# A dense expert stage on one Trainium2 core: VectorE takes every third weight tile's low part instead of every second

## The chip, the cores and the metric

The kernel runs on one NeuronCore of a Trainium2 chip. The metric is the device time of one execution in microseconds (us), median over runs. The profile is of one execution, with times from the start of its span.

Engines: TensorE (PE) multiplies, VectorE (DVE), ScalarE (ACT) and GpSimd (POOL) do elementwise work, SyncE (SP) issues most DMAs. GpSimd also issues the indirect DMAs, which gather rows.

## The reference

Two layers in fp32 on 512 tokens (528 with 16 meta tokens) of width 1024. The first is latent attention beside a convolution, then a feed-forward layer with 16,384 experts; the second mixes sparse latent attention with a recurrent branch. The time around the change goes into the experts:

```
q = (xb @ wq).reshape(C, 8, 2, 64)
s = einsum('chpd,hpnd->chpn', q, keys)          # 8 heads, two halves, 128 keys each
sv, si = top_k(s, 16)                           # then the best 16 of the 16 x 16 sums
g = softmax(top_s)                              # 16 gates for each head
act = gelu(einsum('chkd,cd->chk', u_tab[eidx], xb))
out = einsum('chk,chkd->cd', g * act, v_tab[eidx])
```

Each token uses 128 of the 16,384 rows of u_tab and v_tab.

## The kernel before

**Two ways for the experts.** For the first 128 tokens (and partly for 16 more) the kernel gathers the chosen rows: GpSimd issues an indirect DMA of 128 rows of 1024 numbers (line 2838) into one of six buffers `fetched`, and VectorE multiplies and adds it up. One such row step is a "pick". For the other 368 tokens it computes all experts densely: U products (activations of 128 experts), a gelu on ScalarE, a gating on VectorE (line 2426, times the scattered gates `gr`), and V products. A group is 1024 experts: 8 U tiles and 8 V tiles. There are 16 groups. The U products of nine of them were made earlier and their activations spilled to HBM; SyncE loads these back. In the dense stage the U and V products of group n+1 and n alternate where group n+1 is not spilled (here called a UV stretch, 16 products), and V products stand alone where it is (a V stretch, 8 or 16 products). The stage has 184 products, tiles 100 to 283 of one stream of weight tiles.

**Three-pass products.** A weight tile has 128 x 1024 numbers. SyncE loads it to one of four buffers `wraw`. ScalarE casts it to the high part `wh` (fp32r, line 1330), and another engine makes the low part `wl` = `wraw` - `wh` (one of three buffers each). TensorE then does, for each of eight slices, high x high, high x low and low x high (lines 515 to 517): 24 matmuls. The moving operand of a V product is the gated activations, split in the same way: ScalarE casts WTH (line 1652), VectorE subtracts to get WTL (line 1917, the same helper as for `wl`).

**Who makes the low part.** `on_vector(n)` says whether tile n is VectorE's. `low_of(n)` gives the semaphore that TensorE and SyncE wait on, `w_lo_dve` or `w_lo`. VectorE's `split_lo` (line 1919) and GpSimd's (line 2714) both run through the tiles and each skips the other's.

**What orders the work.** Each engine goes through the same list of steps (`EXPERTS`), in order, waiting on semaphores:

- ScalarE: the high part of tile n waits for the load and for the end of product n-3, whose buffers it takes. It stands in order behind WTH casts and gelus.
- GpSimd: at product p the low part of tile p+2, if it is its own (waits for the high part), and then the gathers of that step, asked for four picks ahead (`LEAD`), each after the pick that last used the buffer.
- VectorE: at product p the low part of tile p+2, if its own; at a V product it then waits for the product's end, adds it to `h`, makes one or two WTL of the next group, and does the picks (`PICKS_AT`: about 1.7 for a product in UV stretches, 1.2 in V stretches). At a U step it does the gating.
- SyncE: the load of tile n waits for the low part of tile n-4.
- TensorE: product n waits for high and low part of tile n; the first V product of a group also for WTH and WTL.

Of the kernel before, what the change touches and what calls it, by code (L numbers as in the profile page):

```python
# [58 lines left out]
W_IN, W_OUT, W_Q, W_SPILL, W_EXP = 0, 12, 20, 28, 28 + 8 * SPILLED  # L59
W_IDX = W_EXP + 8 * (N_GROUPS - SPILLED) + 8 * N_GROUPS  # L60
# [82 lines left out]
def build_program(nc, hT, wstream, gains, consts, trig, w_uq, w_ukv, keys, w_uk, w_uv, w_rg, u_rows, v_rows, out):  # L143
# [319 lines left out]

    def on_vector(n):

        return n < 3 or W_EXP + 10 <= n < W_IDX and n % 2 == 1

    def low_of(n):
        return (w_lo_dve if on_vector(n) else w_lo).at(n)
# [1415 lines left out]
    def vector(dve):  # L1885
# [33 lines left out]
        def split_lo(n):  # L1919
            if on_vector(n):  # L1920
                dve.wait_ge(*w_hi.at(n))
                minus_high(wl[n % NSPLIT][:, :], wraw[n % NRAW][:, :], wh[n % NSPLIT][:, :]).then_inc(*w_lo_dve.tell(n))
# [785 lines left out]
    def gpsimd(pool):  # L2708
# [5 lines left out]
        def split_lo(n):  # L2714
            if n >= N_TILES:
                return
            s, r = n % NSPLIT, n % NRAW
            if on_vector(n):
                return
            pool.wait_ge(*w_hi.at(n))  # L2720
            minus_high(wl[s][:, :], wraw[r][:, :], wh[s][:, :]).then_inc(*w_lo.tell(n))
# [422 lines left out]
```

## Time and profile before

| | |
|---|---|
| median of 3 runs | 2054.63 us (2053.85 to 2056.38) |
| the profiled execution | 2055.25 us, span 2053.3 us |
| TensorE busy | 2016.6 us (98%) |
| VectorE busy | 1508.6 us (73%) |
| ScalarE busy | 994.3 us (48%) |
| GpSimd busy | 1049.1 us (51%) |

Engine busy times are sums of the spans of their instructions. Matmuls overlap, so a busy TensorE may still lose a little; its stalls are seen in its timeline as the idle time in brackets. An instruction that is held up by another engine on a shared resource is shown as busy and long, not as waiting.

### The profile page before, as it was taken

How to read it: one execution, taken by the hardware profiler on the slowest of the kernel's cores; microseconds unless marked ns; L12 is line 12 of the kernel's file. 1: busy time of each engine (PE TensorE's matmuls, PEld its weight loads, DVE VectorE, ACT ScalarE, POOL GpSimd, SP SyncE). 2: the span in 40 equal slices, each digit the busy share in tenths (PEclk: the TensorE clock that was granted, in tenths of full speed). 3: DMA queues.
4: the chain of work that ended last, by engine and by line, in shares of the span. 5: the costliest groups of instructions: out<-in, count | busy, mean ns of one | idle time of the engine just before them, and what ended most of it. 6: DMA issues, size and time to landing. Idle time of an engine off the chain costs nothing.

```text
span 2053.3 us, 31764 instructions
## 1 busy us (share of the span) xinstructions
PE 2016.6 (98%) x11815; PEld 1804.4 (88%) x11815; DVE 1508.6 (73%) x2840; ACT 994.3 (48%) x1825; POOL 1049.1 (51%) x615
## 2 busy tenths in 40 slices
PE   9999999999999999999999999999999999999998
PEld 8746789999999999999999999999867787877777
DVE  6237548979898479999989999997687645067863
ACT  4337433367789743333333343334556642255643
POOL 3213456764445567776767676673334444411242
PEclk9999999999999999999999999999999999999999
DMA  5330225776678899999999999996312222210021
GB/s 205 81 101 11 76 90 160 252 248 226 216 261 287 312 360 372 378 386 374 355 366 366 380 379 391 354 397 209 123 62 93 88 87 103 95 40 31 21 83 62
DMA packets 152855, 435.31 MB, mean 212 GB/s; under 512 B 14464, under 2 KB 62720, under 8 KB 150528
## 3 DMA queue, kind: packets, MB, share of 16 engines
q1 hardware_dynamic: 111232, 282.29, 38.9%
q0 software_dynamic: 41472, 151.01, 19.6%
q8 instruction: 95, 1.56, 0.3%
q14 instruction: 56, 0.46, 0.1%
HBM read 391.28 MB, written 41.97 MB: 211 GB/s over the span
## 4 chain that ended last, share of the span: by engine, by line
PE 83%; DVE 9%; issue 3%; DMA 2%; ACT 2%; POOL 1%; SPq 0%; DVEq 0%; ACTq 0%
PE bank L515 17%; PE bank L516 16%; PE bank L517 16%; PE bank L921 4%; PE bank L922 4%; PE bank L923 4%; PE bank L902 3%; PE bank L1142 2%; DVE wide L2390 2%; PE bank L690 1%; DMA fetched<-in_v_rows,diag 1%; DVE fetched L2370 1%; PE wide L1165 1%; PE wide L1153 1%; PE bank L1165 1%
## 5 line engine op out<-in xcount | busy, mean ns | idle before, releaser
L2712 POOL TENSOR_TENSOR wl<-wraw,wh 128x1024 fp32r<-128x1024 f32 x272 | 673.7, 2481 | 714.0 <-ACT wh L1330 712.4
L1330 ACT CAST wh<-wraw 128x1024 fp32r<-128x1024 f32 x360 | 375.2, 1045 | 167.2 <-PE bank L517 138.2
L515 PE MATMUL bank<-XH,wh 128*128 128x368 f32 (+2 forms) x976 | 345.0, 353 | 1.2 <-ACT wh L1330 1.1
L515 PE MATMUL bank<-WTH,wh 128*128 128x368 f32 x1024 | 338.0, 330 | 8.2 <-issue 8.2
L516 PE MATMUL bank<-XL,wh 128*128 128x368 f32 (+2 forms) x976 | 341.2, 350 | 0.0
L517 PE MATMUL bank<-XH,wl 128*128 128x368 f32 (+2 forms) x976 | 339.9, 348 | 0.0
L516 PE MATMUL bank<-WTL,wh 128*128 128x368 f32 x1024 | 337.1, 329 | 0.0
L517 PE MATMUL bank<-WTH,wl 128*128 128x368 f32 x1024 | 337.1, 329 | 0.0
L921 PE MATMUL bank<-XH,wh 128*128 128x368 f32 x576 | 196.7, 342 | 8.5 <-issue 3.7
L515 PEld LDWEIGHTS bank<-XH,wh 128*128 128x128 f32 x976 | 183.7, 188 | 23.3 <-issue 4.8
L515 PEld LDWEIGHTS bank<-WTH,wh 128*128 128x128 f32 x1024 | 192.7, 188 | 11.3 <-issue 11.3
L516 PEld LDWEIGHTS bank<-XL,wh 128*128 128x128 f32 x976 | 183.6, 188 | 18.4 <-issue 2.1
L517 PEld LDWEIGHTS bank<-XH,wl 128*128 128x128 f32 x976 | 183.8, 188 | 16.2
L2838 POOL DMA_INDIRECT fetched<-in_u_rows,diag x144 | 162.4, 1128 | 65.2 <-DVE fetched L2370 41.5
L517 PEld LDWEIGHTS bank<-WTH,wl 128*128 128x128 f32 x1024 | 192.7, 188 | 0.0
L516 PEld LDWEIGHTS bank<-WTL,wh 128*128 128x128 f32 x1024 | 192.7, 188 | 0.0
L922 PE MATMUL bank<-XL,wh 128*128 128x368 f32 x576 | 191.8, 333 | 0.0
L923 PE MATMUL bank<-XH,wl 128*128 128x368 f32 x576 | 191.3, 332 | 0.0
L2838 POOL DMA_INDIRECT fetched<-in_v_rows,diag x144 | 150.2, 1043 | 39.1 <-issue 30.6
L2390 DVE SCALAR_TENSOR_TENSOR wide<-fetched,diag,wide 128x1024 f32<-128x1024 f32 x127 | 162.9, 1283 | 7.9 <-DMA fetched<-in_v_rows,diag 4.3
L921 PEld LDWEIGHTS bank<-XH,wh 128*128 128x128 f32 x576 | 109.6, 190 | 11.8 <-issue 10.7
L1917 DVE TENSOR_TENSOR wl<-wraw,wh 128x1024 fp32r<-128x1024 f32 (+1 forms) x92 | 110.3, 1199 | 2.5 <-ACT wh L1330 2.5
(552 smaller groups left out, 3862.1 us busy)
## 6 DMA issues: line engine op xcount, KB each, us to landing
wraw<-in_wstream SPq DMA_DIRECT2D x360, 512.0 KB, 5.0
g_scratch<-gs SPq DMA_DIRECT2D x12, 2048.0 KB, 9.0
gr<-g_scratch SPq DMA_DIRECT2D x15, 1536.0 KB, 10.8
a_scratch<-tmp SPq DMA_DIRECT2D x72, 184.0 KB, 2.7
tmp<-a_scratch SPq DMA_DIRECT2D x46, 184.0 KB, 7.7
sq<-a_scratch SPq DMA_DIRECT2D x26, 184.0 KB, 7.6
shifted<-hc_scratch SPq DMA_DIRECT2D x12, 270.0 KB, 4.8
fetched<-in_u_rows,diag POOLq DMA_INDIRECT x144, 7.8
```

Of the source, the lines that this page charges most:

```text
L515: pe.matmul(o, w1, x1, start=n == 0, stop=False)
L516: pe.matmul(o, w1, x2, start=False, stop=False)
L517: m = pe.matmul(o, w2, x1, start=False, stop=n == len(ks) - 1)
L902: mm = pe.matmul(bank[:, i * 128:i * 128 + 128], hots[q % 4][1][:, i, :], hots[q % 4][0][:, i, :], start=True, stop=True, skip_group_check ...
L921: pe.matmul(o, w1s[:, c:c + 128], XH[:, k, FETCH + EXTRA:S], start=k == 0, stop=False)
L922: pe.matmul(o, w1s[:, c:c + 128], XL[:, k, FETCH + EXTRA:S], start=False, stop=False)
L923: mm = pe.matmul(o, w2s[:, c:c + 128], XH[:, k, FETCH + EXTRA:S], start=False, stop=k == KT - 1)
L1330: act.copy(wh[n % NSPLIT][:, :], wraw[n % NRAW][:, :]).then_inc(*w_hi.tell(n))
L1917: return dve.tensor_tensor(lo, src, hi.bitcast(F32), ALU.subtract)
L2390: dve.scalar_tensor_tensor(wide[1][:, :], flat, eweight[:, s:s + 1], wide[1][:, :], ALU.mult, ALU.add).then_inc(*picked.tell(("v", s)))
L2712: return pool.tensor_tensor(lo, src, hi.bitcast(F32), ALU.subtract)
L2838: pool.indirect_dma_start(fetched[buf][:, :], None, u_rows if what in ("u", "u2") else v_rows, bass.IndirectOffsetOnAxis(ap=(eidx if what ...
```

## The change

Between tile 110 and tile 283, VectorE takes the tiles with n % 3 == 1 instead of the odd ones. GpSimd takes the others. Nothing else is touched; both `split_lo` and `low_of` follow `on_vector`.

```diff
     def on_vector(n):
 
-        return n < 3 or W_EXP + 10 <= n < W_IDX and n % 2 == 1
+        return n < 3 or W_EXP + 10 <= n < W_IDX and n % 3 == 1
 
     def low_of(n):
         return (w_lo_dve if on_vector(n) else w_lo).at(n)
```

W_EXP is 100 and W_IDX is 284.

## Rows read from the trace of the kernel before

**Rows 1.** Waits in the dense stage (703 to 1456 us): waiter, awaited, us, times, longest.
```profile
PE bank L515 <- issue: 8.2, 9, 1.7
...
ACT wh L1330 <- DMA wraw<-in_wstream: 0.8, 1, 0.8
```

**Rows 2.** Timeline of TensorE: start, duration, line, operation, [idle before].
```profile
704.41 0.41 PE L515 MATMUL bank<-XH,wh 128*128 128x368 f32 x1
...
837.57 0.41 PE L515 MATMUL bank<-WTH,wh 128*128 128x368 f32 x1 [0.45 <-issue]
...
907.79 0.33 PE L515 MATMUL bank<-WTH,wh 128*128 128x368 f32 x1
...
972.64 0.41 PE L515 MATMUL bank<-WTH,wh 128*128 128x368 f32 x1 [0.64 <-issue]
...
1070.72 0.41 PE L515 MATMUL bank<-WTH,wh 128*128 128x368 f32 x1 [0.74 <-issue]
...
1169.77 0.41 PE L515 MATMUL bank<-WTH,wh 128*128 128x368 f32 x1 [1.68 <-issue]
...
1397.74 0.41 PE L515 MATMUL bank<-WTH,wh 128*128 128x368 f32 x1 [0.74 <-issue]
```

**Rows 3.** Timeline of GpSimd, in a UV and in a V stretch.
```profile
898.79 1.96 POOL L2838 DMA_INDIRECT fetched<-in_u_rows,diag  x1 [0.30 <-issue]
...
902.59 2.40 POOL L2712 TENSOR_TENSOR wl<-wraw,wh 128x1024 fp32r<-128x1024 f32 x1 [0.61 <-ACT wh L1330]
...
1167.31 2.36 POOL L2712 TENSOR_TENSOR wl<-wraw,wh 128x1024 fp32r<-128x1024 f32 x1 [4.09 <-ACT wh L1330]
```

**Rows 4.** Timeline of ScalarE before the stall at 1169.77.
```profile
1165.77 0.50 ACT L1652 CAST WTH<-tmp 128x368 fp32r<-128x368 f32 x1 [8.54 <-DVE tmp L2426]
1166.18 1.05 ACT L1330 CAST wh<-wraw 128x1024 fp32r<-128x1024 f32 x1
```

**Rows 5.** Timeline of VectorE, in the same two stretches.
```profile
898.72 1.21 DVE L1917 TENSOR_TENSOR wl<-wraw,wh 128x1024 fp32r<-128x1024 f32 x1
900.47 0.56 DVE L2426 TENSOR_TENSOR tmp<-tmp,gr 128x384 f32<-128x384 f32 x1 [0.54 <-ACT tmp L1662]
...
904.42 0.97 DVE L1917 TENSOR_TENSOR WTL<-tmp,WTH 128x368 fp32r<-128x368 f32 x1
...
1166.57 0.53 DVE L1917 TENSOR_TENSOR WTL<-tmp,WTH 128x368 fp32r<-128x368 f32 x1
1167.65 2.41 DVE L1917 TENSOR_TENSOR WTL<-tmp,WTH 128x368 fp32r<-128x368 f32 x1 [0.55 <-ACT WTH L1652]
```

**Rows 6.** Windows (a UV, a V stretch): length, busy us by engine, clock, DMA.
```profile
875.70:939.90 64.20, 64.20 (x386) 64.20 (x386) 58.38 (x89) 23.66 (x32) 50.73 (x34) 1.00 1.00 384
1061.80:1094.80 33.00, 32.26 (x194) 31.98 (x193) 31.89 (x38) 11.04 (x16) 20.54 (x14) 1.00 0.97 369
```

**Rows 7.** Groups of instructions, 703 to 1456 us: count, busy us, mean ns, idle before.
```profile
L2712 POOL TENSOR_TENSOR wl<-wraw,wh 128x1024 fp32r<-128x1024 f32 x98 | 245.2, 2504 | 178.1 <-ACT wh L1330 177.7
...
L1917 DVE TENSOR_TENSOR wl<-wraw,wh 128x1024 fp32r<-128x1024 f32 x87 | 106.3, 1222 | 2.5 <-ACT wh L1330 2.5
```

**Rows 8.** Windows, VectorE's WTL subtractions (L1917) alone: dense stage, a V stretch.
```profile
703.00:1456.00 753.00, 119.29 (x128) 1.00 0.94 355
...
1061.80:1094.80 33.00, 6.08 (x8) 1.00 0.97 369
```

**Rows 9.** Windows, VectorE's gatings (L2426) alone: dense stage, a V stretch.
```profile
703.00:1456.00 753.00, 93.00 (x128) 1.00 0.94 355
...
1061.80:1094.80 33.00, 7.42 (x8) 1.00 0.97 369
```

**Rows 10.** Windows, GpSimd's gather issues (L2838) alone: dense stage, a UV stretch.
```profile
703.00:1456.00 753.00, 265.63 (x246) 1.00 0.94 355
875.70:939.90 64.20, 31.44 (x26) 1.00 1.00 384
```

**Rows 11.** All gathers in the dense stage, from issue to landing.
```profile
DMA to landing us min/median/max: 5.1/7.9/12.9
```

## The prediction

> **What bounds the kernel now.** The page's busy shares come first (table above): TensorE 98% of the span. The change touches only tiles of the dense expert stage, from its first product at 704.41 us [rows 2] to about 1456 us: 184 products of 24 matmuls, 4.0 us each. Next the waits of that stage: TensorE stood still 8.2 us in nine places [rows 1]. That is all that faster low parts can give back here, since the matmuls stay.
>
> The timeline of TensorE shows the places, the first at 837.57, the last at 1397.74, nine in all [rows 2]. Counted from 704.41 us they open tiles 133, 134, 166, 190, 206, 214, 215, 246 and 270. Eight of them lie early in a stretch of eight or sixteen V products without U products between ("V stretch"); only 206 lies where U and V alternate ("UV stretch"). At tile 214 the stall of 1.68 us ends at 1169.77; GpSimd's low part of the tile ran from 1167.31 to 1169.67 [rows 3]. It had waited 4.09 us for ScalarE's high part (1166.18, 1.05 us), and that stood behind the cast of WTH, which waited 8.54 us for VectorE's gating [rows 4]. So a late VectorE delays the high part, and the low part comes last. VectorE is busy 31.89 of 33.00 us in a V stretch and 58.38 of 64.20 us in a UV stretch; GpSimd 20.54 and 50.73 [rows 6].
>
> **The change part by part.** Of tiles 110 to 283 VectorE now has the 87 odd ones, afterwards 58. Counted out, 58 odd ones leave it and 29 even ones come. GpSimd then has two tiles in a row, VectorE the third. Count, shape and order of the matmuls, high parts and loads stay.
>
> *Off VectorE:* 29 x 1.222 = 35.4 us. *Onto GpSimd:* 29 x 2.504 = 72.6 us [rows 7]. Neither is on the path by itself; it acts through who is late.
>
> *GpSimd blocks VectorE.* The WTL subtraction takes 0.53 us undisturbed (1166.57) and 2.41 us at 1167.65: it ends once GpSimd's subtraction is over, plus its own time [rows 3, 5]. In the stage 128 of them took 119.29 us [rows 8], 51 more than at 0.53; 128 gatings 93.00 us [rows 9], 23 more than at 0.55. That is 74 us over 98 low parts of GpSimd, 0.76 us each. If each of 29 more costs as much, VectorE loses 22 us again and its relief is 13 us. Bounds: without more blocking 35 us. In the V stretch from 1061.8, 8 WTL took 6.08 us and 8 gatings 7.42 us [rows 8, 9], 4.9 us too much over 4 low parts, 1.2 us each: no relief at all. In UV stretches it can turn to a loss. Today all of GpSimd's low parts there belong to V tiles and straddle the end of a V product; they hit WTL (0.97 us at 904.42 beside a low part from 902.59 to 904.99) and spare the gating (0.56 at 900.47) [rows 3, 5]. With two in a row both are hit, the second one 1 us longer. Per pair of products WTL is held up 0.45 to 0.55 us now; then (0 + 0.55 + 1.6)/3 = 0.7, and the gating as much, 1.4 us. Over eight pairs +7 us against 2.67 x 1.22 = 3.3 us of relief: VectorE would carry up to 4 us more. I take no relief and no loss in UV stretches, between 35/6 and -4 us for each.
>
> *VectorE blocks GpSimd's gathers.* One issued beside VectorE's low part (898.72, 1.21 us) takes 1.96 us [rows 3, 5]; 246 took 265.63 us [rows 10], 34 more than at 0.94, 0.40 us for each of 87 low parts. So much comes back for each tile that moves.
> The Trainium skill ("SBUF — State Buffer", Who interferes with whom) holds that a `tensor_tensor` with two SBUF inputs blocks GpSimd's reads, but, as an inference, not descriptor generation, which needs the write interface. Row 898.79 differs: the issue is doubled just beside such an instruction. By the page the 0.40 us would not come back, and GpSimd would stand at 65.0 us instead of 63.9 in the next sum.
>
> *GpSimd in a UV stretch:* 50.73 us busy, and 26 gather issues [rows 6, 10] each with 0.30 us of "issue" before it [rows 3], 7.8 us: 58.5 of 64.2 us. Added 2.67 x (2.41 - 0.40) = 5.4: 63.9 us. It is full. A product with a low part and two gathers takes it 2.41 + 0.15 + 2 x 1.24 = 5.04 us against 4.0, so the second low part of two in a row starts 1.0 us late, and so do the gathers behind it. The low parts bear that: one ended at 904.99 and its product started at 907.79 [rows 2, 3], 2.8 us to spare. The gathers have less: they land 7.9 us after issue in the median, 12.9 us at most [rows 11], and are asked for four picks, some 9 us of products, ahead. I let VectorE slip by the same 1.0 us by the end of a UV stretch. Six V stretches with a stall follow (at tiles 134, 166, 190, 214, 246, 270): 6.0 us. The one UV stretch that stalls already (206) gets 1.0 us once. Bounds of these 7.0 us: 0, if VectorE's relief pays for the slip, and double. In V stretches GpSimd has room: 20.54 + 10 x 0.30 = 23.5 of 33 us, and 1.33 x 2.4 = 3.2 more.
>
> *Stalls that go:* 166, 190 and 214 move to VectorE, whose low part is 1.2 us shorter and isn't blocked; its gating is done by 1166.1 and the high part at 1167.2 [rows 4], so it is there in time. Gain 0.64 + 0.74 + 1.2 = 2.6 us [rows 2]; at least 0, at most the 8.2. 133 stays on VectorE, 134, 206, 246 and 270 on GpSimd; 215 goes to GpSimd, which has room there: 0.
>
> *Loads:* SyncE loads tile n+4 once the low part of n is done. A GpSimd low part is up to 2.4 us later; ScalarE waited 0.8 us for loads in the whole stage [rows 1], so the distance of four tiles hides it. If that cover went, each delayed load would hold up the high part by up to 2.4 us. Priced at 0; no byte is added, though the DMA engines are at a share of 0.97 to 1.00 [rows 6].
>
> Sum: -2.6 + 6.0 + 1.0 = +4.4 us on the profiled execution's 2055.25 us (span 2053.3 and 1.95 around it), 2059.65. That execution stands 0.6 us above the median of the runs; against 2054.63 the change gives 2059.0.
>
> **The rivals.**
> *Relief decides (faster).* VectorE is behind eight of nine stalls, and 35 us leave it. For: it is busy 31.89 of 33.00 us in a V stretch, while GpSimd has idle time there. Against: the measured blocking gives most of it back. If the net 13 us, about 1 us for each group of products between two boundaries, cancel the slip, the 7 us vanish and most of the 8.2 us of stalls go: -3 to -8, about 2049.
> *VectorE blocked twice in UV stretches (clearly slower).* If two low parts in a row lie over gating and WTL as worked out, VectorE ends each of six UV stretches up to 4 us late and pays at the boundary: 6 x 4.1 - 2.6 = +22, 2077; with half of it 2065. It decides once this load passes what is idle in a UV stretch, 64.20 - 58.38 = 5.8 us [rows 6], of which a part is forced waiting for TensorE. For: GpSimd is full, so the second low part can't be early.
> *No net effect.* The stalls only change tiles: 2054 to 2056.
> The Trainium skill ("Perfetto Trace Analysis", Optimizing Scalar/DVE Operations) warns that moving work between these two engines might not help, because they share a port; that is this last rival, and the 74 us of excess speak for it.
>
> **How the numbers follow.** A measurement of this kernel can tell about 0.2%, 4.1 us, from no change. Forecast 0.48: its own range is 0 to +9 us, 2054.6 to 2063.6, and as it stands at the bound, half of it counts as slower, half as same. Relief 0.27, nearly all faster (0.25). Blocked twice 0.18, slower. No effect 0.07, same. Together faster 0.25, same 0.33, slower 0.42. For 8 in 10 the low end takes in most of the relief's -8, 2047, and the high end the larger part of the slower rival, 2070.
>
> **What would show it.** Right: 127 low parts on GpSimd and 58 on VectorE in the stage; GpSimd's busy and issue time near 64 us in a UV stretch; gatings there above 0.56 us; stalls at 166, 190 and 214 small and at the other boundaries longer; TensorE's stalls in all near 12 us. Wrong: stalls under 6 us; WTL and gating excess still at 74 us; gathers issued as early as now. Stalls by the dozen inside UV stretches would speak for the slower rival.

## The result

The changed kernel takes 2086.97 us (median of 4 runs, 2086.57 to 2088.80) against 2054.98 us before: ratio 1.0158, 95% interval 1.0146 to 1.0170. It is 32 us slower. The forecast was 2059 us within 2047 to 2070; the time lies outside, on the side of the rival "VectorE blocked twice in UV stretches". All times here are medians of whole executions; one of the four with `LEAD` 5 took 5418 us and is left out of its median.

### The profile page after: what moved, and what is told of

The parts are those of the page before. It is cut to its first block, busy times and chain, and to the rows that moved or that the text cites. A ratio compares the mean times of both kernels' runs of the same rounds, so it can differ in the third digit from the quotient of the medians.

```text
span 2084.9 us, 31764 instructions
## 1 busy us (share of the span) xinstructions
PE 2029.6 (97%) x11815; PEld 1807.7 (87%) x11815; DVE 1541.3 (74%) x2811; ACT 990.3 (47%) x1825; POOL 1111.7 (53%) x644
## 4 chain that ended last, share of the span: by engine, by line
PE 67%; DVE 21%; issue 4%; DMA 3%; ACT 3%; POOL 1%; SPq 0%; DVEq 0%; ACTq 0%
PE bank L515 12%; PE bank L516 11%; PE bank L517 11%; DVE wide L2390 5%; PE bank L921 4%; PE bank L922 4%; PE bank L923 4%; DVE WTL L1917 4%; PE bank L902 3%; DVE fetched L2370 2%; PE bank L1142 2%; DMA fetched<-in_v_rows,diag 1%; PE bank L690 1%; DVE tmp L2426 1%; POOL wl L2712 1%
## 5 line engine op out<-in xcount | busy, mean ns | idle before, releaser
L2712 POOL TENSOR_TENSOR wl<-wraw,wh 128x1024 fp32r<-128x1024 f32 x301 | 740.0, 2462 | 672.0 <-ACT wh L1330 669.8
L2838 POOL DMA_INDIRECT fetched<-in_u_rows,diag x144 | 159.4, 1107 | 66.2 <-DVE fetched L2370 43.1
L2838 POOL DMA_INDIRECT fetched<-in_v_rows,diag x144 | 149.4, 1038 | 49.0 <-issue 22.9
L1652 ACT CAST WTH<-tmp 128x368 fp32r<-128x368 f32 x72 | 36.0, 500 | 222.3 <-DVE tmp L2426 218.7
```

The source lines that it names most:

```text
L2712: return pool.tensor_tensor(lo, src, hi.bitcast(F32), ALU.subtract)
L2838: pool.indirect_dma_start(fetched[buf][:, :], None, u_rows if what in ("u", "u2") else v_rows, bass.IndirectOffsetOnAxis(ap=(eidx if what ...
```

## The profile after

The lists of waits in the stage (now 703 to about 1488 us), which answer [rows 1]:

```profile
PE bank L515 <- issue: 28.3, 24, 5.2
...
POOL fetched L2838 <- DVE wide L2390: 18.3, 19, 2.3
...
POOL fetched L2838 <- DVE fetched L2370: 8.8, 19, 1.8
...
ACT wh L1330 <- DMA wraw<-in_wstream: 0.4, 1, 0.4
```

TensorE stands still 28.3 us in 24 places instead of 8.2 us in nine. Twelve of the 24 lie inside UV stretches (11.2 us), where one did before (0.4 us). Loads are no cause: ScalarE waits 0.4 us for them. New is GpSimd's waiting for VectorE's picks ahead of a gather.

Windows over a UV and a V stretch (length, then busy us of PE, PEld, DVE, ACT, POOL), to set against [rows 6]:

```profile
876.00:943.00 67.00, 64.96 (x384) 63.70 (x383) 62.44 (x84) 20.93 (x30) 55.52 (x37) 1.00 0.98 367
1061.00:1095.00 34.00, 32.93 (x192) 31.67 (x191) 32.51 (x36) 10.04 (x14) 24.68 (x17) 1.00 0.98 366
```

The UV stretch grew from 64.2 to about 67 us. VectorE has less work of its own in it and is busy 62.4 us instead of 58.4. GpSimd is busy 55.5 us, with 26 gaps of 0.30 us 63.3 of the 67.

The groups of low parts, and the sums of VectorE's WTL subtractions, its gatings and GpSimd's gather issues in the stage (three windows, each of those instructions alone), which answer [rows 7], [rows 8], [rows 9] and [rows 10]:

```profile
L2712 POOL TENSOR_TENSOR wl<-wraw,wh 128x1024 fp32r<-128x1024 f32 x127 | 311.6, 2455 | 137.8 <-ACT wh L1330 136.8
...
L1917 DVE TENSOR_TENSOR wl<-wraw,wh 128x1024 fp32r<-128x1024 f32 x58 | 72.9, 1257 | 5.8 <-ACT wh L1330 5.8
```

```profile
703.00:1488.00 785.00, 141.35 (x128) 0.99 0.92 340
```

```profile
703.00:1488.00 785.00, 134.82 (x128) 0.99 0.92 340
```

```profile
703.00:1488.00 785.00, 262.01 (x246) 0.99 0.92 340
```

The counts are as planned. Against 0.53 and 0.55 us for an undisturbed one, the 128 WTL subtractions took 73.5 us too much (51.5 before) and the 128 gatings 64.4 (22.6 before). This excess is called the hold-up below: it went from 74 to 138 us. VectorE gave away 29 x 1.22 = 35.4 us of work and got 63.9 us of hold-up for it: 28.5 us net, beside 32 us measured.

How it looks in a timeline. VectorE, then GpSimd, in a UV stretch of the changed kernel:

```profile
896.21 2.70 DVE L2426 TENSOR_TENSOR tmp<-tmp,gr 128x384 f32<-128x384 f32 x1
...
901.11 1.21 DVE L1917 TENSOR_TENSOR wl<-wraw,wh 128x1024 fp32r<-128x1024 f32 x1
902.25 0.53 DVE L2441 TENSOR_TENSOR h<-bank,h 128x368 f32<-128x368 f32 x1
902.70 3.27 DVE L1917 TENSOR_TENSOR WTL<-tmp,WTH 128x368 fp32r<-128x368 f32 x1
```

```profile
896.09 2.39 POOL L2712 TENSOR_TENSOR wl<-wraw,wh 128x1024 fp32r<-128x1024 f32 x1
...
901.28 1.86 POOL L2838 DMA_INDIRECT fetched<-in_u_rows,diag  x1 [0.30 <-DVE fetched L2370]
903.16 2.39 POOL L2712 TENSOR_TENSOR wl<-wraw,wh 128x1024 fp32r<-128x1024 f32 x1
```

GpSimd's low part starts 0.12 us before the gating. The gating, 0.56 us in the same kind of place before [rows 5], takes 2.70: the whole low part and then its own time. Seven us later the next low part of GpSimd holds up WTL until 905.97. Both were predicted to be hit in UV stretches; here they are.

Not every instruction beside a low part is held up. A few us later, GpSimd first, then VectorE:

```profile
909.14 2.40 POOL L2712 TENSOR_TENSOR wl<-wraw,wh 128x1024 fp32r<-128x1024 f32 x1 [0.76 <-ACT wh L1330]
```

```profile
909.78 0.53 DVE L2441 TENSOR_TENSOR h<-bank,h 128x368 f32<-128x368 f32 x1
910.23 1.70 DVE L1917 TENSOR_TENSOR WTL<-tmp,WTH 128x368 fp32r<-128x368 f32 x1
```

The addition to `h` passes in its 0.53 us, and WTL behind it waits for the low part's end. In the kernel's code `bank` and `wide` are PSUM tiles, so the addition and the picks read only one operand from SBUF; WTL reads two. In the whole stage of the changed kernel, 37 such additions and 42 of the common picks (lines 2370 and 2390) start inside a low part, at least 0.3 us before its end, and none takes longer than elsewhere (at most 0.54, 1.22 and 1.29 us). The 35 WTL and 44 gatings that do so take 1.86 and 1.96 us on average.

And the chain of work that ended last now runs over VectorE alone in that stretch, where before it was TensorE's matmuls:

```profile
894.00 2.28 DVE fetched L2370 x4
896.28 2.62 DVE tmp L2426
898.91 2.28 DVE fetched L2370 x4
901.19 1.14 DVE wl L1917
902.33 0.45 DVE h L2441
902.78 3.19 DVE WTL L1917
905.97 1.14 DVE fetched L2370 x2
```

Where the time went by stretch, from the starts of the products in TensorE's timeline: the six UV stretches took 386 us before and 406 after (64.2 to 65.1 each, then 66.3 to 70.0), the V stretches from tile 108 to the end of the last product 334 and 347. The stage as a whole grew by 33.3 us.

## The experiments

Theory A: GpSimd's low parts hold up those instructions of VectorE that read two operands from SBUF (WTL, gating and its own low part); VectorE's lateness goes over gating, WTH cast and high part to the product. Rivals: B, only the amount of work that changes hands matters; C, VectorE's low parts in V stretches; D, GpSimd itself is full, so low parts and gathers come late.

### Where the change hurts

The first two use the third pattern in only one kind of stretch (`in_uv` holds the tiles of the UV stretches).

```diff
+        return n < 3 or W_EXP + 10 <= n < W_IDX and (n % 3 == 1 if n in in_uv else n % 2 == 1)
```

> Every third tile on VectorE only in the UV stretches (96 tiles), every second one elsewhere. Theory A (GpSimd's low parts hold up VectorE's gating and WTL subtractions; in the UV stretches they newly hit the gating): the six UV stretches carry their +20 us (64.2 to 67.3 us each) and what their backlog costs behind them, so about +20 to +27 us over before, 2075 to 2082. Rival B (only the share of work matters, equally everywhere): 96 of 174 tiles, so about 17 of the 32 us, 2072, and the rest comes with the V stretches. Rival C (VectorE's low part being on the path in the V stretches matters most): under 2065.

```diff
+        return n < 3 or W_EXP + 10 <= n < W_IDX and (n % 2 == 1 if n in in_uv else n % 3 == 1)
```

> Every third tile on VectorE only in the V stretches (78 tiles), every second one in the UV stretches. Theory A: the V stretches had low parts over both gating and WTL before as well, so moving 13 tiles there adds little beyond its own relief: -2 to +6 us, 2053 to 2061. Rival B: 78 of 174 tiles, +14 us, 2069. Rival C: +20 us and more.

Measured: 2078.89 us in UV stretches only (ratio 1.0115, 1.0098 to 1.0131), 2066.61 us in V stretches only (1.0057, 1.0040 to 1.0074), before beside them 2055.47. The two parts, +23.4 and +11.1 us, add up to about the whole. Counted from the pattern, 15 and 14 low parts change sides (the expected texts say 13 for the V stretches and, further below, 16 for the UV stretches). The pattern in the UV stretches carries two thirds, as A said. In V stretches it costs more than A's -2 to +6. The hold-up tells why: it is 113 us in the first run and 99 in the second, against 74 before. That is 2.6 us for each low part moved in UV stretches and 1.8 us for each in V stretches, both more than the 1.22 us that it takes off VectorE. C wanted the first under 2065 us and is out; B's 17 and 14 us fit worse than A.

The time is not lost only where the pattern changed. In the first run the UV stretches are 12 us longer in all, and the V stretches, whose tiles are as before, 11 us: VectorE carries its lateness over the boundary.

### GpSimd busy without reading

In the changed kernel and in the one before, GpSimd's low parts of tiles 110 to 283 are replaced by writing zeros.

```diff
+            if W_EXP + 10 <= n < W_IDX:
+                for x, cols in enumerate((1024, 1024, 480)):
+                    if x:
+                        pool.wait_ge(*blank.at(n, x - 1))
+                    m = pool.memset(wl[s][:, 0:cols].bitcast(F32), 0.0)
+                    m.then_inc(*(w_lo.tell(n) if x == 2 else blank.tell((n, x))))
+                return
```

> The changed kernel, but GpSimd writes zeros three times (1024, 1024 and 480 columns) into the low part buffer instead of subtracting, for tiles 110 to 283: it leaves out those low parts, takes GpSimd about the same 2.4 us, and reads nothing from SBUF. Theory A (GpSimd's reading holds up VectorE): gating back to 0.56 and WTL to 0.53 us, VectorE is relieved by 29 x 1.22 us and 138 us of holding up, TensorE stalls nearly vanish: 2045 to 2050. Rival D (GpSimd is full, so low parts and gathers come late whatever it does): it stays within 8 us of 2087. If writing holds VectorE up as well, gating and WTL stay long and the time stays too; then A and D aren't told apart by the time but by GpSimd's delays.

> The kernel before (odd tiles on VectorE), with the same replacement: GpSimd writes zeros three times instead of subtracting for its tiles of 110 to 283, which leaves those low parts out. Theory A: VectorE loses the 74 us of holding up, TensorE's 8.2 us of stalls vanish but for a remainder: 2045 to 2049, and the changed pattern with zeros is no slower than this one. Rival D (GpSimd's occupancy sets the time): the difference between the two patterns stays near 32 us with zeros too.

Measured: 2045.83 us with the third pattern (0.9956, 0.9939 to 0.9972) and 2045.22 us with the odd tiles (0.9951, 0.9935 to 0.9968). With GpSimd no longer reading, the 32 us between the two patterns are gone, and both are faster than the kernel before. The timelines of VectorE and GpSimd in the first of them:

```profile
902.11 0.53 DVE L1918 TENSOR_TENSOR WTL<-tmp,WTH 128x368 fp32r<-128x368 f32 x1
...
904.84 1.22 DVE L1918 TENSOR_TENSOR wl<-wraw,wh 128x1024 fp32r<-128x1024 f32 x1
906.19 0.56 DVE L2427 TENSOR_TENSOR tmp<-tmp,gr 128x384 f32<-128x384 f32 x1
```

```profile
901.04 2.54 POOL L2726 MEMSET wl<- 128x1024 f32 x3
903.74 0.94 POOL L2846 DMA_INDIRECT fetched<-in_u_rows,diag  x1 [0.16 <-issue]
904.99 1.88 POOL L2846 DMA_INDIRECT fetched<-in_u_rows,diag  x1 [0.31 <-DVE fetched L2371]
```

GpSimd is busy from 901.04 to 903.58, as long as with a low part, and WTL passes beside it in 0.53 us. Over the stage, the 128 WTL took 67.52 us and the 128 gatings 70.31: 0.53 and 0.55 each, no hold-up at all. The windows of each one's own stage, of the changed kernel and then of this one, and last a UV stretch of this one:

```profile
702.70:1488.20 785.50, 756.47 (x4452) 744.88 (x4451) 703.65 (x811) 282.99 (x398) 572.51 (x373) 0.99 0.92 340
```

```profile
704.50:1446.90 742.40, 742.34 (x4452) 741.16 (x4452) 564.22 (x811) 290.12 (x399) 565.58 (x605) 1.00 0.95 360
...
875.80:940.00 64.20, 64.20 (x386) 64.20 (x385) 51.97 (x90) 23.62 (x32) 52.77 (x58) 1.00 1.00 380
```

GpSimd is busy 565.6 of 742.4 us here (76%) against 572.5 of 785.5 (73%), and the kernel is 41 us faster. In the UV stretch it has 52.8 us and 26 gaps of 0.30, 60.6 of 64.2 us, the same 94% as 63.3 of 67. So D doesn't explain the 32 us: a GpSimd that is as full costs nothing while nothing is held up. Nor is it that the memset comes in three pieces: low parts in two and four pieces that still read, tried below, leave more than half of the hold-up. The Trainium skill ("SBUF — State Buffer", Who interferes with whom) says that VectorE with two SBUF inputs contends with a GpSimd instruction that reads SBUF, not with one that only writes. These rows agree (0.53 us beside the memset, 3.27 us beside a low part). The same section infers that a `tensor_tensor` doesn't hold up descriptor generation, the work of issuing a gather. Here the measurement differs: a gather issued 0.15 us after the start of VectorE's low part (904.99 and 904.84) takes 1.88 us instead of 0.94.

The pair also shows that relieving VectorE by 35 us brings nothing once the stalls are gone: 2045.8 against 2045.2.

### Same share, other tiles

```diff
+        return n < 3 or W_EXP + 10 <= n < W_IDX and n % 2 == 0
```

> VectorE takes the even tiles of 110 to 283 instead of the odd ones: the same share as before, 87 each, but in the UV stretches GpSimd's low parts now belong to U tiles. Theory A in its form by place (in UV stretches a low part of a V tile straddles the end of a V product and holds up WTL, that of a U tile the end of a U product and holds up the gating): gating long and WTL short in UV stretches, the sum of both as before or somewhat above, 2052 to 2062. Rival B (only the share counts): 2054 to 2056. If placing is what made the change slow, it shows here as over 2065.

Measured: 2098.07 us (1.0209, 1.0192 to 1.0226). The same 87 tiles on each engine, and 43 us slower: which tiles matters more than how many, and B is out. But my form of A by place was wrong in the detail. Not the gating was held up (92.05 us for 128, as before) but WTL: 162.52 us against 119.29. And TensorE waits directly for high parts, GpSimd for picks:

```profile
POOL fetched L2838 <- DVE wide L2390: 64.3, 69, 2.3
...
POOL fetched L2838 <- DVE fetched L2370: 25.5, 38, 2.1
POOL fetched L2838 <- issue: 22.0, 82, 0.3
PE bank L515 <- issue: 20.5, 17, 2.2
...
PE bank L515 <- ACT wh L1330: 15.1, 7, 3.3
```

The 90 us of waiting for picks (10 us before) point to a second path, which follows from the order of the code: a late VectorE holds up GpSimd's gathers, which stand ahead of GpSimd's next low part.

### More work on VectorE

```diff
+        return n < 3 or W_EXP + 10 <= n < W_IDX and n % 3 != 1
```

> VectorE takes two of three tiles (n % 3 != 1, 116 of 174), GpSimd one: the other direction from before. Theory A with 1.2 to 2.2 us of holding up for each low part on GpSimd against 1.22 us of work on VectorE: VectorE gains 29 x (0.8 to 2.2) - 35 = -12 to +28 us, so 2048 to 2062, near before or faster. Rival B/E (VectorE is full and only its own work counts): +35 us of VectorE work, 2075 to 2090.

Measured: 2064.55 us (1.0048, 1.0031 to 1.0065). That is 2.6 us above A's range: the hold-up fell only to 60 us (WTL 116.54, gating 81.77 us), 14 us less for 35 us of work more. Of the three shares tried, half and half is the fastest.

### Fifteen tiles more on GpSimd, none in return

```diff
+        return n < 3 or W_EXP + 10 <= n < W_IDX and (n % 2 == 1 and (n not in in_uv or n % 3 != 0))
```

> The kernel before, but in the UV stretches every third of VectorE's odd tiles goes to GpSimd too (16 tiles), and VectorE takes none in return; V stretches as before. If the net number of tiles on GpSimd decides (the third pattern has the same net 16 there), +23 us as with the third pattern in UV stretches only, 2078. If it is which tiles (a new low part of a U tile holds up, and VectorE's even tiles make it worse), only half as many tiles change hands and it is +5 to +14 us, 2060 to 2069. Under +3 us would say that VectorE's own even tiles are what costs.

Measured: 2068.16 us (1.0069, 1.0053 to 1.0086), +13.9 us. The third pattern in UV stretches has the same net 15 tiles and costs 23.4. So both count: 15 more tiles on GpSimd, though they take 18 us of work off VectorE, cost 14 us, and exchanging another 17 odd ones against even ones costs 9 more.

### When gathers are asked for

In the changed kernel, `LEAD` 5 and then 3 instead of 4.

```diff
-EARLY_PICKS, LEAD, NEARLY, NFETCH = 42, 4, 3, 6
+EARLY_PICKS, LEAD, NEARLY, NFETCH = 42, 5, 3, 6
```

> The changed kernel with gathers asked for five picks ahead instead of four. Rival D in its form by gathers (VectorE slips because rows land late): the rows come some 2.4 us earlier, VectorE's 17 us of waiting for rows go and most of the 32 us with them, 2058 to 2070. Theory A: only those waits go and the rest is holding up, which doesn't change: 2080 to 2087.

> The changed kernel with gathers asked three picks ahead instead of four. With five it waited 121 us for picks and ran 2121 us. If GpSimd's waits for VectorE's picks (31 us in the changed kernel) feed the lateness back, they go, and it is faster than 2087 by 3 to 12 us unless rows then land late. If rows land late (they take 8 us, three picks are some 7 us), VectorE waits for them by tens of us and it is slower, 2095 and more.

Measured: 2120.71 us with five (median of three executions; 1.0323, 1.0302 to 1.0344), 2102.58 us with three (1.0232, 1.0215 to 1.0249). Both are slower than the 2087 of four; neither A nor D had 2121. With five (703 to 1500 us):

```profile
POOL wl L2712 <- ACT wh L1330: 80.5, 48, 6.1
POOL fetched L2838 <- DVE wide L2390: 71.7, 62, 3.5
PE bank L515 <- issue: 50.5, 52, 3.3
...
POOL fetched L2838 <- DVE fetched L2370: 37.0, 39, 2.7
```

GpSimd reaches a gather before VectorE's pick has freed its buffer and stands there, 121 us in all its forms, with the next low part behind it. TensorE loses 50.5 us. With three, these waits shrink to 17 us, but VectorE waits 41 us for rows (21.2, 18.1 and 1.9), as the second case of the expected text said. With five ahead, lateness comes back through GpSimd; in the even tiles the same waits are seen; how much of the changed kernel's 32 us goes that way (31 us of such waits, 12 before) the run with three can't tell, because it brings the other wait.

### Shorter instructions on GpSimd

The low part in two or four instructions, so that VectorE may get in between.

```diff
+            cuts = 2 if W_EXP + 10 <= n < W_IDX else 1
+            for x in range(cuts):
+                c = slice(1024 // cuts * x, 1024 // cuts * (x + 1))
+                m = minus_high(wl[s][:, c], wraw[r][:, c], wh[s][:, c])
+            m.then_inc(*w_lo.tell(n))
```

> The kernel before (odd tiles on VectorE), but each low part of GpSimd for tiles 110 to 283 is made in two instructions of 512 columns. Theory A (one instruction of GpSimd holds VectorE up to its end, at most 2.4 us): a hold-up ends after at most 1.2 us if VectorE gets in between, so the 74 us of holding up fall to 35 to 50 and the 8.2 us of stalls to 2 to 5: 2049 to 2052. If GpSimd's next piece always comes first, nothing changes: 2054 to 2057. Rival D (GpSimd's time): a little slower by the extra instruction's overhead, 2055 to 2060.

> As the first, in four instructions of 256 columns. Theory A: holding up under 35 us; but each instruction adds overhead on GpSimd (some 0.1 us, 9 us in the stage for each extra piece of 87), which shows in its busy time. 2047 to 2053. If VectorE is now held up by more pieces in a row, or its own instructions hold up GpSimd's pieces more often, it is no better than two pieces.

> The changed kernel (every third tile on VectorE) with GpSimd's low parts in two instructions of 512 columns. Theory A: the 138 us of holding up fall to 65 to 95 and about half of the 32 us comes back, 2065 to 2075. Rival D: GpSimd has more to do, 2087 or slower.

Measured: 2057.86 us with two pieces (1.0017, 1.0008 to 1.0026), 2060.94 us with four (1.0029, 1.0019 to 1.0040), and 2092.74 us for the changed kernel with two (1.0187, 1.0171 to 1.0202). All three miss A's numbers. Where D had a number, it is met: 2055 to 2060 for two pieces, 2087 or slower for the changed kernel. The hold-up did fall, from 74 to 57 us with two and to 39 us with four pieces, and from 138 to 124 us in the changed kernel. But a low part became longer, 2.80 and 3.31 us instead of 2.50, and where it is the last link before the product, that counts in full. Four pieces, timelines of GpSimd and TensorE at tile 134:

```profile
841.25 3.41 POOL L2712 TENSOR_TENSOR wl<-wraw,wh 128x256 fp32r<-128x256 f32 x4 [4.69 <-ACT wh L1330]
```

```profile
844.76 0.41 PE L515 MATMUL bank<-WTH,wh 128*128 128x368 f32 x1 [2.79 <-issue]
```

So A needs an addition that is D's in a small form: the hold-up makes VectorE late, but the stall at a boundary has the low part's own length in it.

### The high part ahead of the WTH cast

ScalarE's order at the start of a V stretch: the high part goes before the first WTH cast instead of the second.

```diff
-                elif i > 0:
+                elif i != 1:
                     stream()
```

> The kernel before, with one order changed on ScalarE: at the start of a V stretch the high part of the third V product's tile is cast before the first WTH cast of the next group, not behind it, so it no longer waits for VectorE's gating. Theory A with its path (late gating, then WTH cast, high part, low part, product): of the nine stalls the six at the third V product go (166, 190, 214, 246, 270 and 134), 7 of 8.2 us, 2047 to 2051. If the stalls have another cause (the low part or GpSimd itself late), 2054 to 2056.

> The changed kernel with the same order. Theory A: the late high parts at the starts of V stretches are 5 to 12 us of its 32 us; the rest is VectorE's backlog inside the stretches (gating and WTL held up), where this order does nothing: 2073 to 2083. Rival D (GpSimd full): under 3 us of gain, 2084 to 2088. If over 20 us come back, the path through ScalarE's order at the boundary was nearly all of it.

Measured: 2049.11 us for the kernel before with this order (0.9969, 0.9958 to 0.9981), 2074.66 us for the changed kernel with it (1.0090, 1.0075 to 1.0105). Both inside A's ranges. In the first, the wait of TensorE is down from 8.2 us in nine places, and the V stretches from 334 to 326 us:

```profile
PE bank L515 <- issue: 2.8, 5, 1.3
```

That shows the path over gating, WTH cast and high part at the boundary: it was 6.9 us of the kernel before and 12 to 14 us of the changed one (by the times, and by the ratios to the kernel before beside each). Between the two patterns 26 of the 32 us stay, so only some 6 us of the difference went this way. The kernel with this order and the odd tiles beats both kernels, by 0.31% and 1.8%.

## Why the prediction was wrong

**What bounds: right.** All that happened lies in the dense stage; the stalls at the third V product of a group (134, 166, 190, 214, 246, 270) have the cause that was read from [rows 3] and [rows 4], shown by the reordered kernel. Two of them, 166 and 246, aren't early in their stretch, as the prediction says, but in its second group.

**The failed step.** "I take no relief and no loss in UV stretches, between 35/6 and -4 us for each." The working in front of it had +7 us of hold-up and 3.3 us of relief for each UV stretch, up to 4 us of loss. Measured were 46 us more hold-up in the six (WTL 33 to 51, gating 0.5 to 28.5), 7.6 us each, and 3.3 us longer stretches. The worked-out number was right. I set it aside and took 0, between it and the relief that the mean over the stage gave (0.76 us for each low part). That mean came from a pattern whose low parts spare the gating in UV stretches; it doesn't carry over to a pattern in which they don't. In the sum this left only 1.0 us of slip for each boundary, 7.0 us in all, where the third pattern in UV stretches alone cost 23.4. The rival built on the number had a chance of 0.18, and the range stopped at 2070, short of its own 2077.

**V stretches.** "In V stretches GpSimd has room" was true and beside the point. The hold-up there rose from 41 to 58 us for 14 low parts more, 1.3 us each, a little over my upper bound of 1.2 us; with the pattern changed in V stretches alone it was 1.8. The sum had nothing for them, and neither had the rival's +22 us; the pattern in V stretches alone cost 11 us.

**GpSimd full.** The sum of 63.9 us was good (63.3 measured, in a stretch that had grown to 67), but the slip of 1.0 us at each boundary that I derived from it isn't what happened: with zeros written, GpSimd has the same 94% of a UV stretch and nothing slips.

**Gathers.** 0.40 us given back for each tile moved, 11.6 us in all: measured 3.6 (265.6 to 262.0 us). The prediction put all of the gathers' excess on VectorE's low parts. By the timelines 24.0 us of it lay on gathers that overlap one, and 10.6 us on gathers that overlap WTL or a gating; in the changed kernel it is 17.3 and 13.5 us.

**Stalls that go.** 166, 190 and 214 went to VectorE; their products start 0, 0.26 and 0 us late instead of 0.64, 0.74 and 1.68: right, and worth 2.8 us among the 28.3.

**Loads.** Hidden, as priced.

**Not foreseen** is the way back through GpSimd, whose gathers wait for VectorE's picks (31 us, 12 before), and TensorE's clock below. The stalls came to 28.3 us, not the 12 that the prediction had as a sign of being right, and a dozen of them in UV stretches was its sign for the slower rival.

**Open** is how the 32 us divide between lateness that goes over ScalarE and lateness that goes over GpSimd, beyond the 6 us at the boundaries; and why the exchange of even for odd tiles holds up WTL so much (1.27 us for each instead of 0.93). The sum of VectorE's own low parts and its hold-up goes with the time in four kernels: +30, +22, +8 and +44 us against +32, +23, +11 and +43 (the changed one, the pattern in UV and in V stretches alone, the even tiles). In five it doesn't. With fifteen tiles more on GpSimd it is +1 against +14, in two and four pieces -16 and -31 against +3 and +6, and in the changed kernel with two pieces +23 against +38. With two thirds on VectorE it is +23 against only +10. The first four have more or longer low parts on GpSimd, the last fewer, so GpSimd's own time seems to count beside the hold-up; no run here separates the two.

## What to carry to other kernels

Before moving elementwise work from VectorE to GpSimd, list VectorE's instructions with two SBUF inputs (one SBUF and one PSUM input passed freely here) and see where GpSimd's reading instruction would fall beside them: here each low part moved took 1.22 us off VectorE and put 2.2 us of waiting on it. A mean hold-up holds only for the pattern it was measured in; when the pattern shifts against the other engine's sequence, go by the worked-out overlap. To tell a busy engine from a blocking one, let it do something equally long that doesn't read.

## What the hardware showed beside

TensorE's clock fell beside the three longest stalls, which did not happen in the dense stage before, where the longest was 1.7 us. After the stall of 5.20 us that ended at 1426.99 in the changed kernel, these windows of TensorE alone (length, busy, granted clock, DMA share, GB/s) show half the clock, 1.2 instead of 2.4 GHz:

```profile
1417.00:1421.00 4.00, 4.00 (x26) 1.00 1.03 405
1427.00:1429.00 2.00, 2.00 (x7) 0.50 0.52 137
1429.00:1431.00 2.00, 2.00 (x8) 0.50 1.02 373
```

Matmuls there start 0.31 us apart instead of 0.17. The same was seen after the stalls of 3.04 us (ended at 1246.06) and 1.99 us (ended at 1192.08), where the clock fell 1.2 and 0.6 us after work had resumed. Some 14, 10 and 10 matmuls ran at half the clock, 34 x 0.14 = 4.8 us. With the 20.1 us of standing still more, that is 25 of the 33.3 us by which the stage grew. The other 8 lie mostly in the products on the two sides of a stall, some 0.1 to 0.25 us in each. Consecutive matmuls overlap by 0.16 us, and a stall breaks that overlap, which the brackets don't show.

VectorE's low part holds up a gather that starts behind it. In the kernel before, gathers that start 0.07, 0.45 and 0.85 us after such a low part take 1.96, 1.58 and 1.18 us, so each ends about 2.03 us after the low part's start, whenever it began. Of the 35 that start ahead of a low part and overlap it, 30 keep their 0.94.

In the other direction a VectorE instruction was held up though it began before GpSimd's low part: the WTL of 902.70 shown above, 0.46 us ahead of the low part at 903.16, while GpSimd was issuing a gather (901.28 to 903.14). Gathers alone don't do this: 87 WTL and gatings of the changed kernel overlap a gather and no low part, and none takes more than 0.60 us. What happened in that half microsecond stays open.
